# Three key projections of a decoder layer as seven block products each, with the bias tables built later

## The reference

```python
h = rmsnorm(x, norm_mix[l])
proj = h @ w_in[l]
q_a, kv_a, g_a, qkv_b, g_m = jnp.split(proj, IN_SPLITS, axis=-1)
...
qkv_b = qkv_b.reshape(B, S, 3, len(DIL_GROUPS), DIL_HPG, HEAD_DIM)
for gidx, (window, dil) in enumerate(DIL_GROUPS):
    o_g, lse_g = dilated_group(qkv_b[:, :, 0, gidx], qkv_b[:, :, 1, gidx],
                               qkv_b[:, :, 2, gidx], window, dil, slopes_dil[gidx])
```

## Time and profile before

| | |
|---|---|
| Median of 3 runs | 774.25 us (772.69 to 775.11) |
| The profiled execution | 772.77 us |
| Its span, first to last instruction | 771.0 us |
| Granted TensorE clock, mean | 0.998 of full speed |
| Busy: PE / DVE / ACT / POOL | 99% / 70% / 45% / 21% |

### The profile page before, as it was taken

How to read it: one execution, slowest core, us unless ns; L and a number is a source line. 1 busy time by engine, 2 the same in 40 slices (tenths; PEclk the granted TensorE clock), 3 DMA queues, 4 the chain that set the end, 5 groups by cost and what they waited for, 6 DMA issues and landing times.

```text
span 771.0 us, 13506 instructions
## 1 busy us (share of the span) xinstructions
PE 761.5 (99%) x5426; PEld 681.1 (88%) x5426; DVE 541.2 (70%) x1011; ACT 346.4 (45%) x634; POOL 162.4 (21%) x121
## 2 busy tenths in 40 slices
PE   9999999999999999999999999999999999999996
PEld 7878899889887787788888988999999999999995
DVE  5935432554875777656724769899999998799865
ACT  6212055254456566753323733444444444455434
POOL 1300100000000000001310085877666663000000
PEclk9999999999999999999999999999999999999999
DMA  7941336250311110126331623244433322334532
GB/s 236 347 139 55 110 60 160 58 160 13 111 55 57 56 56 13 30 54 183 140 130 54 205 75 105 79 123 124 114 110 111 110 83 67 105 104 158 178 102 110
DMA packets 104636, 83.59 MB, mean 108 GB/s; under 512 B 16976, under 2 KB 94848, under 8 KB 104576
## 3 DMA queue, kind: packets, MB, share of 16 engines
q1 hardware_dynamic: 104336, 82.46, 35.8%
q10 hardware_dynamic: 240, 0.29, 0.1%
HBM read 77.44 MB, written 5.29 MB: 107 GB/s over the span
## 4 chain that ended last, share of the span: by engine, by line
PE 96%; DVE 2%; issue 1%; POOL 1%; ACT 0%; DVEq 0%; ACTq 0%; POOLq 0%
PE bank L1941 25%; PE bank L1942 25%; PE bank L1943 25%; PE bank L2174 3%; PE bank L2193 2%; PE bank L2414 2%; PE bank L2415 2%; PE bank L2413 2%; PE bank L2161 2%; PE bank L2075 1%; PE bank L2116 1%; PE bank L2097 1%; PE bank L2038 1%; PE bank L1965 1%; PE bank L1982 1%
## 5 line engine op out<-in xcount | busy, mean ns | idle before, releaser
L1191 DVE TENSOR_TENSOR w_lo<-w_raw,w_hi 128x2048 fp32r<-128x2048 f32 (+2 forms) x29 | 64.5, 2224 | 79.8 <-ACT w_hi L760 79.8
L1941 PE MATMUL bank<-n_hi,w_hi 128*128 128x512 f32 x272 | 108.8, 400 | 0.0
L1943 PE MATMUL bank<-n_hi,w_lo 128*128 128x512 f32 x272 | 106.1, 390 | 0.0
L1942 PE MATMUL bank<-n_lo,w_hi 128*128 128x512 f32 x272 | 106.0, 390 | 0.0
L760 ACT CAST w_hi<-w_raw 128x2048 fp32r<-128x2048 f32 (+2 forms) x29 | 53.6, 1849 | 61.8 <-PE bank L1943 50.9
L708 POOL TENSOR_TENSOR n_lo<-merge_tmp,n_hi 128x512 fp32r<-128x512 f32 x8 | 10.4, 1298 | 298.2 <-ACT n_hi L942 298.2
L1941 PE MATMUL bank<-w_hi,n_hi 128*128 128x256 f32 (+2 forms) x192 | 62.1, 323 | 0.0
L1943 PE MATMUL bank<-w_hi,n_lo 128*128 128x256 f32 (+2 forms) x192 | 61.4, 320 | 0.0
L1942 PE MATMUL bank<-w_lo,n_hi 128*128 128x256 f32 (+2 forms) x192 | 61.4, 320 | 0.0
L1943 PEld LDWEIGHTS bank<-n_hi,w_lo 128*128 128x128 f32 x272 | 51.1, 188 | 10.9
L1941 PEld LDWEIGHTS bank<-n_hi,w_hi 128*128 128x128 f32 x272 | 51.1, 188 | 10.7 <-issue 1.0
(11 more groups left out here) (321 smaller groups left out, 2241.8 us busy)
## 6 DMA issues: line engine op xcount, KB each, us to landing
w_raw<-in_w_ffn_in_dram SPq DMA_DIRECT2D x44, 512.0 KB, 5.0
w_raw<-in_w_in_dram SPq DMA_DIRECT2D x37, 512.0 KB, 4.7
w_raw<-in_w_ffn_out_dram SPq DMA_DIRECT2D x22, 512.0 KB, 3.5
w_raw<-in_w_out_dram SPq DMA_DIRECT2D x8, 512.0 KB, 4.0
w_raw<-in_w_in_dram SPq DMA_DIRECT2D x12, 256.0 KB, 4.5
xs<-in_x_dram SPq DMA_DIRECT2D x4, 512.0 KB, 5.1
wck_k<-in_w_ck_dram SPq DMA_DIRECT2D x1, 2048.0 KB, 11.9
wck_v<-in_w_cv_dram SPq DMA_DIRECT2D x1, 2048.0 KB, 13.6
```

The lines of the kernel that those rows point to most:

```text
L1191: dve.tensor_tensor(wlo[u % 2][:, split_part(u)], raw[u % 2][:, 0:n], whi[u % 2][:, split_part(u)].bitcast(F32), ALU.subtract).then_inc(lo ...
L1941: pe.matmul(dst, w[0], x_[0], start=start, stop=False)
L1942: pe.matmul(dst, w[0], x_[1], start=False, stop=False)
L1943: return pe.matmul(dst, w[1], x_[0], start=False, stop=stop)
```

## The change

**What it does.** The two tiles of each key unit (4 to 6) are replaced by a job `keys(u)`: seven block products of 128 columns x 256 tokens, over 512 rows each. A block product is 4 steps x 3 matmuls of 256 columns: 12 matmuls, 84 per unit, where two tiles had 48 of 512 columns. The weight side needs one 1024 x 128 half (`wk_hi`, `wk_lo`) and one 512 x 128 block (`wk22_...`) as they are, and four sums (`weight_sums` on POOL, then `sums_hi` on ACT and `sums_lo` on DVE). The input side needs four mixtures of blocks of the normalised input (`n_mixed`), made once by DVE in ten two-source operations, cast by ACT and given low parts by DVE. The results are added up by DVE (`keys`, `keys_out`).

**What it moves.** The four mixtures are made by DVE between the evacuations of tiles 4, 5, 6 and 7. POOL's sums of the first key unit wait for tile 5 (the buffer they lie in is that of the low weights of unit 2), those of the second for tile 7. `dil_bias` moves from `cmp_hidden` to the end of the last `keys` job, `cmp_bias` behind tile 18 and `nsa_bias(0)` behind tile 22. The results of unit 6 are added up (`keys_out`) only behind DVE's part of `dil_scores` 0. The feed-forward part only has its semaphore counts shifted.

```diff
-    jobs += [("tile", n) for n in range(FIRST_TILE[U_KB], FIRST_TILE[U_KB + 1])]
-    jobs.append(("cmp_kv", 0))
-    jobs += [("tile", n) for n in range(FIRST_TILE[U_KB + 1], FIRST_TILE[U_VB])]
+    jobs += [("keys", U_KB), ("cmp_kv", 0), ("keys", U_KB + 1), ("keys", U_KB + 2)]
...
+TILE_BANK[FIRST_TILE[U_VB]], TILE_BANK[FIRST_TILE[U_VB] + 1] = 2, 3
...
+            pool.wait_ge(blk_same, 2)
+            for u in KEY_UNITS:
+                if u - 2 in KEY_UNITS:
+                    used = [(m_done, 7 * (u - 2 - U_KB) + v) for v in (5, 5, 6, 7)]
+                else:
+                    used = [unit_used(u - 2), None, None, None]
+                weight_sums(u, u - U_KB, (raw_full[u % 2], raw_count(u)), slot_view(raw, u, KC, 256), used)
...
+                    if n == FIRST_TILE[U_QB + 1]:
+                        key_mixed(2)
+                    elif n == LAST_TILE[U_QB + 1]:
+                        key_mixed(1)
+                        key_mixed(3)
+                    elif n == FIRST_TILE[U_QB + 2]:
+                        key_mixed_lo(2)
+                        key_mixed(0)
+                    elif n == LAST_TILE[U_QB + 2]:
+                        key_sums_lo(U_KB)
...
             def cmp_hidden():
...
-                dil_bias()
+                key_plain_lo(U_KB, 0)
+                key_mixed_lo(1)
+                key_mixed_lo(3)
+                key_plain_lo(U_KB, 1)
+                key_mixed_lo(0)
...
+                if not more:
+                    dil_bias()
...
                     dil_scores(n)
+                    if n == 0:
+                        keys_out(U_KB + 2)
...
+            def keys(u):
...
+                block_product(ps[a + 1][:, 0:256], plain(0, 4), x1)
+                block_product(ps[a][:, 0:256], plain(4, 8), x2_)
+                if k == 0:
+                    tile_evacuated(FIRST_TILE[U_KB] - 1)
+                    pe.wait_ge(t_lo, 3)
...
+                block_product(ps[a + 2][:, 256:512], [v[s][1] for v in (khi7, klo7)], mixed(3))
```

More of the change, by code:

```diff
@@ L100, in sevens, with ready_count @@
 def sevens(u):
-    return sum(v < u for v in SEVEN)
+    return NK + sum(v < u for v in SEVEN)
 def plains(u):
-    return u - sevens(u)
+    return u - sum(v < u for v in SEVEN)
+def ready_count(n):
+    return n - 1 - (2 * NK if n > LAST_TILE[KEY_UNITS[-1]] else 0)
 def out_sevens(n):
@@ L602, in _ @@
                         permute_rows(TILES[n][0] - U_VB - 1)
+                elif job == "keys":
+                    load(n + 2)
                 elif job == "dil_merge":
@@ L812, in tile @@
                 u, a = TILES[n]
-                if a == 0 and u != U_CMP:
+                if u + 1 == U_KB:
+                    if a == 0:
+                        key_plain_hi(U_KB, 0)
+                        for v in (2, 1, 3):
+                            key_mixed_hi(v)
+                    else:
+                        key_mixed_hi(0)
+                        key_plain_hi(U_KB, 1)
+                        key_sums_hi(U_KB)
+                elif a == 0 and u != U_CMP:
                     split_hi(u + 1)
@@ L881, in _ @@
                     tile(n)
+                elif job == "keys":
+                    keys(n)
                 elif job == "cmp_hidden":
@@ L1363, in tile, with of_group @@
                         ins.then_inc(blk_cross, 1)
+            def of_group(to, g, a, src, row):
+                dst = to[:, 2 * g + a, :]
+                if g:
+                    dst = dst.rearrange("p (r t) -> p r t", r=4)
+                    src, row = (v.rearrange("p (t r) -> p r t", r=4) for v in (src, row))
+                return dst, src, row
+            early, late = slice(0, 256), slice(256, 512)
+            first, second = slice(0, 4), slice(4, 8)
+            n_f, n_l = nhi[:].bitcast(F32), nlo[:].bitcast(F32)
@@ new lines, in pair_of, with keys_out @@
+            def pair_of(v):
+                return v.rearrange("p (b c) -> p b c", b=2)
+            def keys_out(u):
+                k, a = u - U_KB, TILE_BANK[FIRST_TILE[u]]
+                dve.wait_ge(u4u3_made, k + 1)
+                dve.wait_ge(m_done, 7 * k + 7)
+                for part in range(2):
+                    bank = ps[a][:] if part == 0 else twin[a // 2 + 1].rearrange("p b c -> p (b c)")[:, 256:768]
+                    added = key_m1u4u3[:, 0:2, :] if part == 0 else key_m1u4u3[:, 2:3, :].to_broadcast([P, 2, 256])
+                    done = up_sums if part else g_sums
+                    dve.tensor_tensor(pair_of(bank), pair_of(bank), added, ALU.add).then_inc(done, 1)
+                    dve.wait_ge(done, k + 1)
+                    dst, src, row = of_group(kb, k, part, bank, rrow[:])
+                    dve.scalar_tensor_tensor(out=dst, in0=src, scalar=1.0, in1=row,
+                                             op0=ALU.mult, op1=ALU.mult).then_inc(tile_evac_dve, 1)
@@ new lines, in keys @@
+            def keys(u):
+                k, a, more = u - U_KB, TILE_BANK[FIRST_TILE[u]], u + 1 in KEY_UNITS
+                if k:
+                    keys_out(u - 1)
+                if more:
+                    key_plain_lo(u + 1, 0)
+                    key_plain_lo(u + 1, 1)
+                dve.wait_ge(m1_out, k + 1)
+                dve.wait_ge(m_done, 7 * k + 4)
+                dve.tensor_tensor(key_u2[:], ps[a + 1][:, 256:512], key_m1u4u3[:, 0, :], ALU.add).then_inc(u2_made, 1)
+                if more:
+                    key_sums_lo(u + 1)
+                else:
+                    split_lo(u + 1)
+                dve.wait_ge(u2_made, k + 1)
+                dve.wait_ge(m_done, 7 * k + 6)
+                if k:
+                    dve.wait_ge(up_sums, k)
+                dve.tensor_tensor(key_m1u4u3[:, 1:3, :], pair_of(ps[a + 3][:]),
+                                  key_u2[:].unsqueeze(1).to_broadcast([P, 2, 256]), ALU.add).then_inc(u4u3_made, 1)
+                if not more:
+                    dil_bias()
@@ L1539, in _ @@
                     tile(n)
+                    if n == FIRST_TILE[U_VB + 1]:
+                        cmp_bias()
+                    elif n == FIRST_TILE[U_VB + 2]:
+                        nsa_bias(0)
+                elif job == "keys":
+                    keys(n)
                 elif job == "cmp_hidden":
```

210 lines of the change are left out of this document (164 added, 46 removed).

## The result

The changed kernel takes 777.34 us (median of 7 executions, 776.37 to 778.39) beside 774.25 for the kernel before (7 executions, 772.38 to 775.56): ratio 1.0049, 95% interval 1.0039 to 1.0060. It is slower by 3.0 to 4.6 us. A second set (5) gave 776.47 beside 773.16, ratio 1.0029 (1.0017 to 1.0041). The prediction was 774.6 us and "same", with "slower" above 776.6; the time lies just inside its range of 771.3 to 777.6, the direction doesn't fit.

The account below looks back on a forecast made before the run. The prediction took PE to set the time: -4.1 us of products, +3.2 and +1.3 of stalls, +0.4 in sum. Against 772.77 us that made 773.2, as a median 774.6 us, with 8 in 10 for 771.3 to 777.6.

Parts of the forecast that it names:

- same: Whole kernel: predicted direction, between faster (below 771.9 us) and slower (above 776.6 us); chance 0.60.
- What goes from PE: Three key units on PE: each takes 9.52 us instead of 10.88, -4.08 us in all.
- Rival C: Key products on PE: 256-column matmuls run at 0.12 us, not 0.113; 776.1 us; chance 0.10.
- What DVE gets, and what POOL does to it: DVE ahead of tile 7: out at 62.1 us alone; alternating with POOL adds 3.0 and 2.2, giving 67.3.
- rival A: DVE ahead of tile 7: POOL costs DVE little, tile 7 out by 64.1; 771.5 us; chance 0.17.
- rival B: PE in the key units: neither stall comes; 770.2 us; chance 0.06.
- First stall: PE before the third product of unit 4 waits for tile 7's bank: +3.2 us, 2.1 to 4.3.
- Between the stalls: Units 4 to 6 after tile 7: low sums, copies and adding up make PE wait for nothing.
- Second stall: PE at tile 16 waits for bank 6, held by unit 6 until `keys_out`: +1.3 us.
- `cmp_bias` and `nsa_bias`: Moved on DVE (1.7 and 1.3 us) to where it will wait for PE anyway: cost nothing.
- rival D: The clock falls in a stall of about 4 us, costing 2 us, or 4 for two stretches; chance 0.12.
- The sum: Whole kernel: -4.1 + 3.2 + 1.3 = +0.4 us, 773.2 us, as a median 774.6.

Follow-up runs that it names:

- 5: The changed kernel run again with no edit, beside the kernel before: 776.47 us beside 773.16, ratio 1.0029.
- 3: The changed kernel with POOL's weight sums of unit 5 held back until tile 7 is evacuated: 779.13 us, ratio 1.0070.
- kernel 1: The changed kernel with 24 matmuls of no use on PE behind the second product of unit 4: 775.19 us, ratio 1.0024.
- 4: The changed kernel with `dil_bias` built earlier, behind the outputs of unit 5: 775.34 us, ratio 1.0027.
- 8: The changed kernel with 2, 4, POOL's unit 5 sums and DVE's low sums later, `nsa_bias` behind the third `dil_scores`: 773.84 us, ratio 1.0004.
- 9: 8 with the first addition of unit 5's outputs ahead of unit 6's low sums and `dil_bias` cut in two: 770.36 us, ratio 0.9950.
- 10: 9 without POOL's wait and with the low sums in the order of the change: 772.45 us, ratio 0.9984.
- 2: The changed kernel with tile 7 evacuated two low parts earlier and half of unit 4's low sums ahead of mixture 0's low part: 774.49 us, ratio 1.0018.
- kernel 6: The kernel before with six, seven or eight additions of no use on DVE ahead of `h_rows`: ratios 1.0038, 1.0060 and 1.0087.

## Why the prediction was right in its stalls and wrong in its answer

- **What goes from PE, -4.1 us.** PE sets the time here: it is busy for 99% of the span, with one wait of 0.7 us. Right where it can be read. Units 5 and 6 bring PE 2.66 us nearer to the kernel before, where 2.72 were due; from one product's first matmul to the next one's it is 0.1133 us per matmul in most, up to 0.122 in the first product of unit 5, and 0.115 on average. Rival C (0.12 throughout) is out; in the second set's profile some products ran at 0.118.
- **What DVE gets, and what POOL does to it: tile 7 out at 67.3.** Right, it was out at 67.7 in an execution that ran 0.4 us late. The mixtures took 1.43 and three times 2.2 beside POOL and 1.23 alone, as the pattern of the earlier trace rows said. The evacuation of tile 7 took 1.05 us beside a sum of POOL's (65.58 to 67.83), no more than before (1.08). The 2.2 us of unit 5's sums were shown by themselves in 3. With that rival A, by which POOL costs DVE little and tile 7 is out by 64.1 (771.5 us), and rival B are out.
- **First stall, +3.2 us.** 2.96. Right as an idle time.
- **Between the stalls, nothing.** Right: PE waits neither for a low sum nor for a copy there. In after the half clock gave DVE more time than was forecast; kernel 1, at the full clock and with the third product from 67.6, has no such wait either. Units 5 and 6 take 9.7 us each.
- **Second stall, +1.3 us.** 1.27, ended by `keys_out`; taking the table out of the row took the stall away (4). One sum on the way is off by 0.1: 1.07 + 48 x 0.12 is 6.83, not 6.95, which would have made the stall 1.4.
- **`cmp_bias` and `nsa_bias`: nothing.** Wrong by 0.5 to 0.8 us. "They go where DVE will wait for PE anyway" holds for `cmp_bias`. `nsa_bias` (1.29 us, from 130.7) stands behind the low part of unit 10 and ahead of the maxima of the fourth `dil_scores`, which start at 132.07. ACT can take these scores only then, and it evacuates a value tile behind them, at 136.1, for whose bank PE waits 0.53 us. Moved up behind `dil_scores` 2, where DVE waits 6.5 us for ACT, it makes no wait: there is none at this place in 8, 9 and 10. I had looked at the engine that runs the step, not at the engine behind it.
- **The clock: the step that failed.** The forecast priced the first stall at its idle time, and rival D let the clock fall only in a stall of about 4 us. That number was my estimate from the earlier trace rows, the one place where the trace of before had idle time long enough: in windows of half a microsecond the clock is 1.00 up to 767.5, 4 us after the last matmul, and 0.55 and 0.50 in the next two. One row was read as a bound. The runs put in its place: with PE idle for 3.0 and 2.9 us the clock fell in both profiles of after, and of its 16 executions nine have a mean of 0.995 or less and four more 0.996; at 4.8 and at 3.6 us it is five of five at 0.995 or less, at 2.9 us (4) five of twelve, at 2.4 us four of ten, at 2.0 us two of twelve, with waits of 0.5 to 1.3 us alone (2) none of eleven, and none of 75 in the kernel before. The wait at the full clock that the earlier trace rows had timed was also of another kind: the program had ended, and no matmul came behind it. The time lost behind the idle time is 1.7 us (3.4 us at the low level) or 3.2 us (6.8 us), where my estimate for rival D was 2 us, or 4 for two such stretches. (With a chance of 0.12 the direction came out as D had it, from a stall of 3.0 us, not of 4.) On average over the executions it is, as an estimate, (0.9974 - 0.9951) x 777 = 1.8 us in the first set, with before's clock taken from the later sets, and 1.1 in the second.

**The sum again**, with what the profiles show: -4.1 + 3.0 + 1.5 (tiles 14 to 16, 1.27 of it the second stall) + 0.8 (around 136.6 us) = +1.2 us, and 1.1 to 1.8 for the clock as an average, so +2.3 to +3.0. The two sets gave +2.2 and +3.8, +-0.9 each. +0.4 had been forecast; the clock is the larger half of the difference, `nsa_bias` most of the other. The changed kernel is slower for its order, not for its arithmetic: with the same instructions in another order and one table in two parts it is 0.5% faster than the kernel before (9).

What stays open: what decides, within one kernel, whether the clock falls in an execution and whether for 3.4 or 6.8 us. It didn't fall at a fixed distance from the start of the idle time: 2.3 us behind it in after and 3.0 in kernel 3, with PE still idle; 3.6 in the second profile of after and 4.0 in kernel 6 with seven additions, where PE had taken up work again; and 4.8 with eight additions, just as PE went on. Nor is the drift of up to 1.0 us in the feed-forward part explained. Kernels 8, 9 and 10 moved several things at once, so the 0.5% of kernel 9 belongs to the order as a whole and is not split up among its parts.
